# Decode value pages in two sets of buffers and three smaller moves in the attention stage of a hybrid decoder step

## What is computed

```python
# prompt: 8 heads of 64, causal, with a decay from cumulated forget gates
s = einsum('bqhd,bkhd->bhqk', qi, k) * scale + ci[..., :, None] - ch[:, :, None, :]
p = softmax(where(kpos <= qpos, s, NEG)); o = einsum('bhqk,bkhd->bqhd', p, v)
# samples: the same for one query against 256 past rows, held in 2 pages of 128 rows per sample
k_past = cache_k[page_table, l]; v_past = cache_v[page_table, l]
```

## Time and profile before

| | us |
|---|---|
| median of three runs | 2101.49 |
| the profiled execution | 2097.6 |
| its span, first to last instruction | 2095.9 |
| PE busy in the span | 2073.0 |
| DVE busy | 1127.0 |
| ACT busy | 703.8 |
| attention from the first key step to the mixer's output product | about 454 to 612 |

### The profile page before, as it was taken

How to read it: one execution, slowest core, us unless ns; L and a number is a source line. 1 busy time by engine, 2 the same in 40 slices (tenths; PEclk the granted TensorE clock), 3 DMA queues, 4 the chain that set the end, 5 groups by cost and what they waited for, 6 DMA issues and landing times.

```text
span 2095.9 us, 37938 instructions
## 1 busy us (share of the span) xinstructions
PE 2073.0 (99%) x17092; PEld 2050.4 (98%) x17092; DVE 1127.0 (54%) x1509; ACT 703.8 (34%) x877; POOL 46.5 (2%) x93
## 2 busy tenths in 40 slices
PE   8999999999999999999999999999999999999999
PEld 8999999999889999999999999999999999999998
DVE  6443244856767544234686443244898854323467
ACT  5221123423344422122344221122487432212243
POOL 0000000021210000000000000000000000000000
PEclk9999999999999999999999999999999999999999
DMA  5222222145331322222222222222222222222222
GB/s 175 88 92 88 96 101 81 63 152 142 126 128 61 104 98 91 91 101 81 100 75 101 99 91 94 98 82 81 82 100 84 81 101 101 82 100 83 99 92 82
DMA packets 35075, 202.81 MB, mean 97 GB/s; under 512 B 5056, under 2 KB 5344, under 8 KB 16992
## 3 DMA queue, kind: packets, MB, share of 16 engines
q1 hardware_dynamic: 29520, 183.87, 24.9%
q0 software_dynamic: 5392, 16.50, 2.5%
HBM read 193.78 MB, written 4.48 MB: 95 GB/s over the span
## 4 chain that ended last, share of the span: by engine, by line
PE 86%; DVE 10%; ACT 2%; DMA 2%; issue 1%; DVEq 0%; POOLq 0%; POOL 0%; ACTq 0%
PE acc L1790 70%; PE acc L1900 10%; DVE w_lo L1085 2%; PE acc L1831 1%; DVE t L1198 1%; DMA raw<-in_weights 1%; DVE x L1205 1%; DVE act_lo L1211 1%; DVE rs_post L1193 1%; PE acc L1980 1%; PE acc L2034 1%; DVE xsum L1220 1%; PE acc L2055 1%; DVE rs_pre L1193 0%; PE acc L2104 0%
## 5 line engine op out<-in xcount | busy, mean ns | idle before, releaser
L1790 PE MATMUL acc<-act_hi,w_hi 128*128 128x260 f32 x3072 | 622.1, 284 | 0.0
L1790 PE MATMUL acc<-act_hi,w_lo 128*128 128x260 f32 x3072 | 618.0, 283 | 0.0
L1790 PE MATMUL acc<-act_lo,w_hi 128*128 128x260 f32 x3072 | 617.7, 283 | 0.0
L1790 PEld LDWEIGHTS acc<-act_hi,w_hi 128*128 128x128 f32 x3072 | 472.9, 188 | 2.7 <-issue 2.0
L1790 PEld LDWEIGHTS acc<-act_hi,w_lo 128*128 128x128 f32 x3072 | 472.9, 188 | 0.4
L1790 PEld LDWEIGHTS acc<-act_lo,w_hi 128*128 128x128 f32 x3072 | 472.4, 188 | 0.5
L690 ACT ACTIVATE w_hi<-raw 128x2048 fp32r<-128x2048 f32 (+3 forms) x179 | 323.0, 1805 | 298.2 <-DMA raw<-in_weights 298.0
L1085 DVE TENSOR_TENSOR w_lo<-raw,w_hi 128x2048 fp32r<-128x2048 f32 (+3 forms) x179 | 386.6, 2160 | 38.2 <-ACT w_hi L690 38.1
L1335 DVE TENSOR_TENSOR gu<-acc,rs_pre 128x520 f32<-128x520 f32 x164 | 114.5, 699 | 440.6 <-PE acc L1790 440.4
L816 ACT ACTIVATE hid_hi<-gu 128x520 fp32r<-128x520 f32 x86 | 55.0, 639 | 476.4 <-DVE gu L1355 476.4
L1790 PE MATMUL acc<-hid_hi,w_hi 128*128 128x260 f32 x1024 | 206.3, 283 | 0.2
(11 more groups left out here) (295 smaller groups left out, 2139.8 us busy)
## 6 DMA issues: line engine op xcount, KB each, us to landing
raw<-in_weights SPq DMA_DIRECT2D x138, 1024.0 KB, 4.8
raw<-in_weights SPq DMA_DIRECT2D x32, 896.0 KB, 4.5
ring<-in_k_pages POOLq DMA_DIRECT2D x16, 256.0 KB, 4.0
ring<-in_v_pages POOLq DMA_DIRECT2D x16, 256.0 KB, 3.7
raw<-in_weights SPq DMA_DIRECT2D x12, 256.0 KB, 5.2
x<-in_x SPq DMA_DIRECT2D x8, 260.0 KB, 6.5
out_y<-x SPq DMA_DIRECT2D x8, 260.0 KB, 2.5
ckb<-ch_rows POOLq DMA_DIRECT2D x8, 256.0 KB, 4.3
```

Source lines behind the costliest of these rows:

```text
L1790: ins = nc.tensor.matmul(a[0:width, half, 0:HALF], w[slot][:, at:at + width], m[:, half * HALF:(half + 1) * HALF], start=first and n == 0, ...
```

## The change

There are four edits.

1. Value pages get a second set of buffers. Value steps 0 and 2 stay in `ring`, steps 1 and 3 go into `xsum`, `ysum`, `rs_post` and unused blocks of `sc` above the diagonal; the page in `sc` needs two DMAs, so such a step has five. POOL starts step 1's pages at h = 2, behind the last key pages; step 2's at h = 4, behind value step 0; step 3's at h = 5, behind value step 1. Nothing of it stands at h = 6 and 7 any more.
2. A value step becomes four parts of eight small matmuls, behind chunks 3, 4, 5 and 6, as a key step is.
3. ACT's `done` for the tiles of head h moves ahead of the exponentials of head h + 1 (the last head's goes behind the loop).
4. PE waits for `pt{h}.2` only ahead of the third block of `pv`, and the transposes of the last head move from chunk 5 to chunk 6 of tile b3.

```diff
+        def spare_page(r, c):
+            if r < RING - 1:
+                return (xsum, ysum, rs_post)[r][:, c * P:(c + 1) * P]
+            return sc[:, 0, (c + 1) * P:(c + 2) * P] if c < AC - 1 else sc[:, 1, 2 * P:3 * P]
+        def value_page(i, r, c):
+            return spare_page(r, c) if i % 2 else ring[:, r, c * P:(c + 1) * P]
...
                         if step:
-                            wait_job(pool, f"{s}.dec_{'so'[(step - 1) // STEPS]}{(step - 1) % STEPS}")
+                            before = step - 2 if step > STEPS else step - 1
+                            wait_job(pool, f"{s}.dec_{'so'[before // STEPS]}{before % STEPS}")
...
+                    def gather_spare(step):
+                        at = step % STEPS * RING
+                        pages = [pool.value_load(table[0:1, n:n + 1], min_val=0, max_val=kpages_d.shape[0] - 1)
+                                 for n in range(at, at + RING)]
+                        if step > STEPS + 1:
+                            wait_job(pool, f"{s}.dec_o{step - STEPS - 2}")
+                        for i, page in enumerate(pages):
+                            whole = vpages_d[bass.ds(page, 1), :, :].rearrange("a p n -> (a p) n")
+                            if i < RING - 1:
+                                pool.dma_start((xsum, ysum, rs_post)[i][:, 0:D_A], whole).then_inc(spare_loaded, 16)
+                            else:
+                                pool.dma_start(sc[:, 0, P:SEQ], whole[:, 0:D_A - P]).then_inc(spare_loaded, 16)
+                                pool.dma_start(sc[:, 1, 2 * P:3 * P], whole[:, D_A - P:D_A]).then_inc(spare_loaded, 16)
...
-                        if h != 4:
-                            gather(h + 1 if h < 4 else h)
+                        if h < 4:
+                            gather(h + 1)
+                        if h == 2:
+                            gather_spare(STEPS + 1)
+                        if h == 4:
+                            gather(STEPS + 2)
+                        if h == 5:
+                            gather_spare(STEPS + 3)
...
                     if h + 1 < HEADS:
+                        for n in tiles_at(s, h):
+                            done(n)
                         exponentials(h + 1)
...
-                    for n in tiles_at(s, h):
-                        done(n)
+                for n in tiles_at(s, MIX_HEAD):
+                    done(n)
...
-                        pe.wait_ge(ring_loaded, 16 * RING * (STEPS + i + 1))
+                        if i % 2:
+                            pe.wait_ge(spare_loaded, 16 * (RING + 1) * (i // 2 + 1))
+                        else:
+                            pe.wait_ge(ring_loaded, 16 * RING * (STEPS + i // 2 + 1))
...
-                    def two_parts(c):
-                        if c in (3, 5):
-                            decode_out(i, c - 3)
-                            decode_out(i, c - 2)
-                    return two_parts
+                    return lambda c: decode_out(i, c - 3) if 3 <= c < 7 else None
...
-                                    lambda c: transposes(MIX_HEAD) if c == 5 else None)
+                                    lambda c: transposes(MIX_HEAD) if c == 6 else None)
...
                     wait_drained(pe, f"{s}.pt{h}.0")
-                    wait_drained(pe, f"{s}.pt{h}.2")
...
                     for kb in range(QB):
+                        if kb == 2:
+                            wait_drained(pe, f"{s}.pt{h}.2")
```

More of the change, by code:

```diff
@@ L450, in trunk @@
         ring_loaded = sem("ring_loaded")
+        spare_loaded = sem("spare_loaded")
         lf_loaded = sem("lf_loaded")
@@ L2054, in decode_out @@
                             src = g * BH + b * HEADS + 2 * c
-                            ins = nc.tensor.matmul(a[:, 0, at:at + 2], ring[:, r + g, c * P:(c + 1) * P],
+                            ins = nc.tensor.matmul(a[:, 0, at:at + 2], value_page(i, r + g, c),
                                                    pT[:, src:src + 2], start=g == 0, stop=g == PAGES - 1)
```

## The result

The kernel after takes 2090.25 us, the median of four runs (2090.0 to 2092.71). The kernel before, run between them, took 2102.37 us (2100.57 to 2105.2). That is a gain of 12.1 us, where 5.4 were predicted. The ratio of the two kernels is 0.9946, with a 95% interval of [0.9931, 0.9961]. The ratios in this document are estimates from all executions of a group and lie up to about 0.001 beside the quotient of the medians, which is 0.9942 here.

The account below looks back on a forecast made before the run. PE bounds the kernel, so only its waits and low clock in the attention stage can be won. 3.19 + 1.24 + 0.44 + 0.5 = 5.4 us, from the median 2101.5 to 2096.1; range 2091.5 to 2102.

Parts of the forecast that it names:

- What bounds the kernel: Whole kernel: PE is busy 2073.0 of 2095.9 us, so only its standstills and low clock can be won.
- Two sets of pages: Value step 3, tile b2: early pages win 3.19 us, 1.64 of wait and 1.55 of low clock; bounds 1.64 and 3.19.
- The step that failed: From profiled execution to median, 3.9 us apart: the same gain put on the median, 2101.5 - 5.4 = 2096.1.
- the rival on the clock: Value steps in singles: clock falls more often, 1.55 us each; one or two falls chance 0.17, four falls 0.04.
- High parts ahead: Between heads 3 and 4: DVE's wait for ACT's high part goes, 1.24 of 1.99 us at head 5's scores.
- Finer wait and last transposes: Ahead of `pv`, four heads at 0.11, 0.44 us; last head's transposes one chunk later, 0.5 us.
- signs of being wrong: In the changed profile: low-clock stretches in x3, b0, b1 or b2, or a new name among PE's waits.
- POOL's move: POOL's gathers at h = 2 and 4: rows and swaps go out later but in time, cost on the path 0.
- Another wait in place of step 3's pages: DVE's chain ahead of head 7's scores, or head 6's softmax, late: 2.2 us remain, 2099.3; chance 0.09.
- ACT's drains costing all of the idle time: Ahead of `pv`: four heads give 3.5 us and not 0.44, 8.5 us in all, 2093.0; chance 0.06.
- Doing nothing: High part waits for its raw unit, or POOL delays a row or swap: no change, 2101.5; chance 0.08.

Follow-up runs that it names:

- the second execution: Kernel before, no edit, profiled and timed again: 2101.64 us, ratio 1.0004; its profiled execution has a span of 2101.4 us.
- the 61 executions: All runs of the unchanged kernel before that the follow-up groups share: 2095.56 to 2106.85 us, mean 2100.5.
- the first execution: Kernel before, no edit, the profiled execution from which the prediction was made: span 2095.9 us, time 2097.6 us.

## Why the prediction was wrong

**What bounds the kernel: right for the execution that was read.** PE's loss by waits and by the clock was the place to look. The gain lies in that stage: 7.43 of the 7.5 us between the spans.

**Two sets of pages: the mechanism right, the term mis-sized.** Tile b2 came to 9.33 us where 9.4 stood in the prediction, and the clock behind value step 3 is up. But the term, 3.19 us, measured 6.9 (4.4 to 9.7) alone. I had worked it out as 12.57 - 9.38 from one execution and let b1 and b0 stand as steps "whose pages were there". In the second execution step 1 waits 2.00 us as well, the clock stays low for some 14 us behind it, and b2 loses 4.9 and not 3.4. By the runs with one step's pages each, step 3 is worth 5.5 us where 3.19 were put, and step 1 about 1.3, not told from 0, where nothing was put.

**The step that failed** is the sentence under the sum: "That execution lies 3.9 us under the median of the three runs, so I put the same gain on the median." Those 3.9 us were not an offset that both kernels share. 1.2 of them were the small sample, since the median of the 61 executions is 2100.3 and not 2101.49. The other 2.7 were more of the same loss, and the change removes that too: the profiled execution of the kernel after is its median, and the pages alone bring 2.6 to 3.7 us more than their term. Had I put all of the 3.9 with the sum, it would have given 2101.5 - 3.9 - 5.4 = 2092.2, which was in the text as the time of the profiled execution. From there to 2090.25 it is 1.9 us, of which 1.57 are the low clock behind key step 3 (1.68 measured, 0.11 predicted). It stands in the first execution; the second passes that stretch in 20.35 us against 21.66, and in the change without the high parts it stands again. So it comes and goes, and no edit is needed to remove it: that this pair of profiles shows it gone is luck of the draw. I took it for a property of the kernel, as the rival on the clock shows.

The first four runs of the kernel before had a median 2.1 us above that of the 61 (2102.37 against 2100.3). Against the 61 the gain is 10.1 us, still nearly twice the prediction. The edits as measured add up to it within their noise: 6.9 for the pages (5.8 by the medians), 1.9 for the high parts and 1.1 for the finer wait are 9.9 (8.8).

**High parts ahead: right.** DVE's low part starts with no wait in front of it. The first row is ACT's high part, behind its drains; the second is ACT's first exponential, still waiting for DVE's maximum; the third is DVE's low part between heads 3 and 4:

```profile
553.16 1.91 ACT L723 ACTIVATE w_hi<-raw 128x2048 fp32r<-128x2048 f32 x1
...
556.07 0.40 ACT L916 ACTIVATE sc<-sc,nmx 128x128 f32<-128x128 f32 x1 [0.99 <-DVE nmx L1547]
...
562.64 2.28 DVE L1120 TENSOR_TENSOR w_lo<-raw,w_hi 128x2048 fp32r<-128x2048 f32 x1
```

The hole of 2.80 us took the high part and 0.99 of it is left. Of the 1.99 us at the scores of head 5, 1.09 stay, where 0.75 were predicted; tile x3's end and the drains have moved too. Without the edit the mixer's output product waits 0.3 us as well, so the waits that go come to 1.6 us; the runs gave 1.9, or 1.4 at a clock of 1.0, against 1.24.

**Finer wait and last transposes: right.** 0.76 us stay ahead of `pv`, as predicted from head 4. The last transposes wait 0.67 us, where 1.25 less 0.715 left 0.53, and 1.1 us were measured against 0.94, inside the noise. The new name in PE's list, 0.3 us for ACT's second pair, is one of the prediction's own signs of being wrong, but its sum already held about 0.2 for that wait.

**POOL's move: right, at nothing.** Its rows at h = 4 and h = 5:

```profile
550.58 2.44 POOL L611 DMA_DIRECT2D ring<-in_v_pages  x4 [23.95 <-PE acc L2093]
...
563.95 0.57 POOL L624 DMA_DIRECT2D xsum<-in_v_pages  x1 [8.35 <-PE acc L2093]
```

Step 3's pages go out from 563.95 on, 17 us earlier than in the earlier trace rows, and no softmax waits for a row.

**The rivals.** More clock falls by the singles: not with the pages there, but 4.2 us slower with the pages late; the rival named the right edit and the wrong condition, and how much of the 4.2 us is the clock wasn't separated. Another wait in place of step 3's pages: none on DVE in tile b2 or at the scores of head 7. ACT's drains costing all of the idle time: no. Doing nothing: no. None of the rivals was that the profile showed a cheap execution, and the range, built from upper bounds of that one execution, ended at 2091.5 for this reason. (It took 1.25 us for the last transposes, whose own bound was 0.72; with that it would have ended near 2092.)

**Open.** Why the clock rises again soon behind some waits and only after 14 us behind others; what makes it fall behind key step 3; how often step 1 loses 6 us; what the 0.76 us ahead of `pv` are.

## What to carry to other kernels

Where the granted clock differs between executions of one kernel, one profile is one draw: hold its time against the median of the timed runs. If it lies below, don't take the difference for an offset that both sides share; here most of it was more of the loss that was being removed. A wait of 2 us can be priced only with the clock behind it, and that price is taken from several executions. A wait for a load can be removed by asking earlier or by moving what loads beside it; here either did, and their prices differ.

## What the hardware showed that I had not expected

After a standstill of about 2 us the clock stayed at 1.2 GHz for some 14 us of unbroken work in the second execution, where in the first execution the low stretch behind a wait of 1.64 us was some 3.5 us long. The length of the wait does not foretell it: 0.96 us had some 10 us of low clock behind them in the kernel with only step 3's pages early. The lower clock lengthens tiny matmuls and their weight loads as it does large ones: sixteen weight loads took 3.53 us against 1.86 in the same trace, ten of the transposes 2.09 against 1.12. And where four pages of 256 KB shared the DMA engines with a weight unit of 1 MB, at step 3 with two stores as well, the slowest of the four took 6.0 to 7.8 us from issue to landing in the two executions of the kernel before; the median of all loads of value pages in each was 3.7.
